# Attention's back steps of a round in one group, retention's two likewise; rotation tiles of q in turn with gate tiles

## What is computed

```python
def second_block(x, ...):
    for l in range(DEPTH_2):
        h = rmsnorm(x, attn_norm[l])
        z = h @ w_in[l]
        (qA, kA, vA, fA, qB, kB, vB, qI, kI, wI,
         qC, kC, vC, gC, qD, kD, vD, gates) = jnp.split(z, split_at, axis=-1)
        yA = forgetting_attention(heads(qA, FOX_HEADS), ...)
        yB = dsa_attention(rope(heads(qB, DSA_HEADS), pos), ...)
        r = retention(rope(heads(qC, RET_HEADS), pos), rope(heads(kC, RET_HEADS), pos) * HEAD_DIM ** -0.5, ...)
        yC = head_groupnorm(r, ret_norm[l]) * jax.nn.silu(gC)
        yD = sliding_window_gqa(rope(heads(qD, SWA_Q_HEADS), pos), ...)
        branch = jnp.einsum('bsnc,ncd->bsnd', jnp.stack([yA, yB, yC, yD], axis=2), w_branch[l])
        merged = jnp.sum(jax.nn.sigmoid(gates) * branch, axis=2)
        x = x + merged @ w_out[l]
        ...
```

## Time and profile before

| | us |
|---|---|
| median of 3 runs | 3758.53 |
| lowest and highest run | 3755.45, 3760.3 |
| the profiled execution, its time | 3764.61 |
| its span in the trace | 3763.2 |

### The profile page before, as it was taken

How to read it: one execution, slowest core, us unless ns; L and a number is a source line. 1 busy time by engine, 2 the same in 40 slices (tenths; PEclk the granted TensorE clock), 3 DMA queues, 4 the chain that set the end, 5 groups by cost and what they waited for, 6 DMA issues and landing times.

```text
span 3763.2 us, 45163 instructions
## 1 busy us (share of the span) xinstructions
PE 3535.7 (94%) x17424; PEld 2778.0 (74%) x17424; DVE 1708.2 (45%) x3133; ACT 1465.7 (39%) x2478; POOL 1419.3 (38%) x651
## 2 busy tenths in 40 slices
PE   6999989897899998999999999998989999989998
PEld 4788889785578876767766778887866766678886
DVE  6876453547420116845542243134755552334133
ACT  3223454554432223344443344343335443334342
POOL 3454433321234443323332344444323332334443
PEclk9999999999999998999999999999999999999999
DMA  7574445221123331212122222323212222223332
GB/s 287 195 249 145 129 155 163 68 85 51 45 80 94 101 93 62 78 45 68 62 82 70 90 73 90 101 93 99 73 51 62 62 68 85 79 79 90 101 94 80
DMA packets 109975, 364.90 MB, mean 97 GB/s; under 512 B 12609, under 2 KB 13505, under 8 KB 109505
## 3 DMA queue, kind: packets, MB, share of 16 engines
q1 hardware_dynamic: 107280, 356.33, 29.5%
q10 hardware_dynamic: 2480, 5.68, 0.4%
HBM read 359.86 MB, written 2.10 MB: 96 GB/s over the span
## 4 chain that ended last, share of the span: by engine, by line
PE 77%; DVE 14%; ACT 5%; issue 2%; DMA 1%; POOL 1%; SPq 0%; DVEq 0%; POOLq 0%; ACTq 0%
PE ps L1308 24%; PE ps L1310 22%; PE ps L1309 22%; PE ps L1552 1%; PE ps L1573 1%; ACT b L1636 1%; DVE b L2171 1%; DVE b L2464 1%; PE ps L1534 1%; DVE b L2463 1%; DVE b L2207 1%; DVE b L2152 1%; POOL b L2535 1%; PE ps L1530 1%; DVE b L2437 1%
## 5 line engine op out<-in xcount | busy, mean ns | idle before, releaser
L2535 POOL TENSOR_TENSOR b<-b,b 128x1024 fp32r<-128x1024 f32 (+2 forms) x579 | 1325.5, 2289 | 2056.2 <-ACT b L1636 2051.1
L1308 PE MATMUL ps<-b,b 128*128 128x512 f32 (+3 forms) x4848 | 1865.9, 385 | 88.9 <-POOL b L2535 26.7
L1310 PE MATMUL ps<-b,b 128*128 128x512 f32 (+3 forms) x4848 | 1804.4, 372 | 0.0
L1309 PE MATMUL ps<-b,b 128*128 128x512 f32 (+3 forms) x4848 | 1804.0, 372 | 0.0
L1308 PEld LDWEIGHTS ps<-b,b 128*128 128x128 f32 x4848 | 934.3, 193 | 357.5 <-issue 147.5
L1310 PEld LDWEIGHTS ps<-b,b 128*128 128x128 f32 x4848 | 934.5, 193 | 161.5
L1309 PEld LDWEIGHTS ps<-b,b 128*128 128x128 f32 x4848 | 936.7, 193 | 145.5 <-issue 5.0
L1636 ACT ACTIVATE b<-b 128x1024 fp32r<-128x1024 f32 (+2 forms) x622 | 607.4, 978 | 269.9 <-PE ps L1310 239.1
L2075 DVE SCALAR_TENSOR_TENSOR b<-ps,b,b 128x511 f32<-128x511 f32 x88 | 66.0, 750 | 371.0 <-ACT b L1687 371.0
L1697 ACT ACTIVATE b<-b 128x512 fp32r<-128x512 f32 (+1 forms) x110 | 64.8, 589 | 391.6 <-DVE b L2084 289.2
L2171 DVE CUSTOM_DVE_ANT_0 b<-b,b,b 128x1024 bf16<-128x1024 f32 x112 | 209.4, 1870 | 17.5 <-DMA b<-in_ada 5.5
(11 more groups left out here) (235 smaller groups left out, 2380.5 us busy)
## 6 DMA issues: line engine op xcount, KB each, us to landing
b<-in_w SPq DMA_DIRECT2D x458, 512.0 KB, 3.5
b<-in_ada SPq DMA_DIRECT2D x88, 512.0 KB, 4.9
b<-in_w SPq DMA_DIRECT2D x80, 384.0 KB, 3.1
b<-in_w SPq DMA_DIRECT2D x80, 320.0 KB, 2.9
b<-in_const SPq DMA_DIRECT2D x24, 256.0 KB, 4.0
b<-in_x SPq DMA_DIRECT2D x1, 2048.0 KB, 16.7
out<-b SPq DMA_DIRECT2D x8, 256.0 KB, 2.5
b<-in_c SPq DMA_DIRECT2D x2, 512.0 KB, 10.1
```

What stands on the lines that cost most here:

```text
L1308: pe.matmul(out, a[0], b[0], start=first, stop=False)
L1309: pe.matmul(out, a[0], b[1], start=False, stop=False)
L1310: return pe.matmul(out, a[1], b[0], start=False, stop=last)
L2535: then(pool.tensor_tensor(wlo[j % NS][:, 0:nk * w], raw[j % NR][:, 0:nk * w], whi[j % NS][:, 0:nk * w].bitcast(F32), ALU.subtract), "lop", j)
```

## The change

Three things are edited. First, the back steps of a round are one item of the list: heads() returns a list [s3, s2, s1] for each round, retention a list [c2, c1], and weave() puts such a list in whole. Second, the rates are changed for that: from 0.8 to 0.31 in A, from 0.6 to 0.235 in B and D, from 0.55 to 0.35 in C, so that a group comes after every fifth k-step in A, every sixth or seventh in B and D, and every fourth or fifth in C, where before single steps came after every second or third. rn1 and rn2 stay single items. Third, in A two gate tiles and one rotated tile of q alternate, four times over, where before four rotated tiles came first; plan() orders the chunks the same way.

```diff
-                cols("gt", w2, l, GT, 1024)
...
-        cols("qb", w2, l, QB, 512)
+        for m in range(4):
+            cols("gt", w2, l, GT + 256 * m, 256)
+            cols("qb", w2, l, QB + 128 * m, 128)
         branch(0)
...
-    def rope(self, name, count, key, **kw):
-        for m in range(count):
+    def rope(self, name, count, key, at=0, **kw):
+        for m in range(at, at + count):
...
-    out, due, back = [], 0.0, list(back)
+    out, due, back = [], 0.0, [b if isinstance(b, list) else [b] for b in back]
...
             if back:
-                out.append(back.pop(0))
-    return out + back
+                out += back.pop(0)
+    return out + [s for b in back for s in b]
...
             for k in range(len(PAIRS) + 3):
-                if k >= 3:
-                    out.append(do("s3", a=kind, l=l, w=k - 3))
-                if 0 <= k - 2 < len(PAIRS):
-                    out.append(do("s2", a=kind, l=l, w=k - 2))
-                if k < len(PAIRS):
-                    out.append(do("s1", a=kind, l=l, w=k))
+                out.append([do(s, a=kind, l=l, w=w) for s, w in (("s3", k - 3), ("s2", k - 2), ("s1", k))
+                            if 0 <= w < len(PAIRS)])
...
-        F.rope("qb", 4, "qb", ver=H, l=l)
-        for m in range(8):
-            t = F.fm("gt", m, "gt", H, L, o=0, l=l)
-            F.step("evac", t=t)
-        S += weave(F, heads("A"), 0.8) + [do("takey", l=l, o=0, t=t) for t in range(4)]
+        for m in range(12):
+            if m % 3 == 2:
+                F.rope("qb", 1, "qb", at=m // 3, ver=H, l=l)
+            else:
+                t = F.fm("gt", m - m // 3, "gt", H, L, o=0, l=l)
+                F.step("evac", t=t)
+        S += weave(F, heads("A"), 0.31) + [do("takey", l=l, o=0, t=t) for t in range(4)]
...
-        S += weave(F, heads("B"), 0.6) + [do("takey", l=l, o=1, t=t) for t in range(4)]
+        S += weave(F, heads("B"), 0.235) + [do("takey", l=l, o=1, t=t) for t in range(4)]
...
-            if k >= 2:
-                B.append(do("c2", l=l, w=k - 2))
-            if k < len(PAIRS):
-                B.append(do("c1", l=l, w=k))
+            B.append([do(c, l=l, w=w) for c, w in (("c2", k - 2), ("c1", k)) if 0 <= w < len(PAIRS)])
```

More of the change, by code:

```diff
@@ L517, in schedule @@
         branch(F, 1, 1)
-        S += weave(F, heads("D"), 0.6) + [do("takey", l=l, o=2, t=t) for t in range(4)]
+        S += weave(F, heads("D"), 0.235) + [do("takey", l=l, o=2, t=t) for t in range(4)]
         F = fore()
@@ L523, in schedule @@
         for k in range(len(PAIRS) + 2):
-            if k >= 2:
-                B.append(do("c2", l=l, w=k - 2))
-            if k < len(PAIRS):
-                B.append(do("c1", l=l, w=k))
+            B.append([do(c, l=l, w=w) for c, w in (("c2", k - 2), ("c1", k)) if 0 <= w < len(PAIRS)])
             if k >= 2 and (k - 2) % 4 == 3:
                 B += [do("rn1", l=l, t=(k - 2) // 4), do("rn2", l=l, t=(k - 2) // 4)]
-        S += weave(F, B, 0.55) + [do("takey", l=l, o=3, t=t) for t in range(4)]
+        S += weave(F, B, 0.35) + [do("takey", l=l, o=3, t=t) for t in range(4)]
         F = fore()
```

## The result

| | us |
|---|---|
| before, median of 4 runs | 3759.41 (3755.45 to 3763.25) |
| after, median of 4 runs | 3826.51 (3824.40 to 3829.37) |
| after / before | 1.017, 95% interval 1.0155 to 1.0185 |
| span of the profiled execution | 3827.9 (before 3763.2) |

The change makes the kernel slower, by 67 us. The forecast was 3802 us with a range from 3768 to 3828: the sign and the mechanism held, the size was 24 us short, and the time lies only 1.5 us inside the upper end.

The account below looks back on a forecast made before the run. Stages were taken as bound by TensorE's issue (busy 94%), leaving only idle time to gain. Per layer 24 + 4 - 2.7 - 4.1 = +21 us, two layers +43 us on the median 3758.5: 3802 us, range 3768 to 3828.

Parts of the forecast that it names:

- rival 3: Slower still: B's starting lag also hits next q tiles' banks and D's start, clock falls every wait; 3826 us, chance 0.08.
- the lag at B's start: The last q rotation, 3.5 us on VectorE, now ends A and delays B; claimed to run through two rotations.
- Where s2 stands: A, B, D: s2 waits for scalings behind rotation parts; 14.4 to 38.5 us, +24 us a layer, bounds 8 and 32.
- R + 4.1: Earliest s2 start behind two to four rotation parts; R: later of tile's end + 0.8 and last maximum + 1.3.
- rival 1: Cover: VectorE reaches the scaling sooner, so new waits vanish and A's go too; -11 us a layer, 3736 us, chance 0.10.
- B's start: First s2 wait in B, behind the last q rotation and takey's subtractions: 3.0 or 7 us, taken as 6.
- Branch tiles: B and D: waits of s2 behind a tile's products (2.9 us) and for its bank (0.9) unchanged: 0, +-3 us.
- The clock: Half-clock stretches after long waits: 13 us lost against 9.5, +4 us a layer, bounds -4 and +12.
- Grouping by itself: s3, s2, s1 in a row save nothing; c2 beside c1 saves a shape change, -2.7 us a layer.
- Rival 2: Format switching: each step away from split fp32 tiles costs, so grouping gives 13 us a layer more; 3776 us, chance 0.06.
- Retention: Stage C: waits before c2's first round and before rn1 and rn2 vanish, -4.1 us; shape changes give -2.7 us.
- A's waits: Sign of being right: waits in stage A near 8 us a layer, against 13.3 before.

Follow-up runs that it names:

- early scaling: The changed kernel with VectorE's scaling of pair k-1 issued directly behind the maximum of s1 of pair k: 3710.4 us.
- short GpSimd operation: The changed kernel with GpSimd's subtraction cut to 16 columns for weight chunks split while a rotated tile's parts run on VectorE: 3767.1 us.
- head steps grouped only: The kernel before with only s3, s2, s1 of a round grouped, at the new spacing; old order of tiles and of retention: 3841.5 us.
- q first: The changed kernel with each q tile of A ahead of its two gate tiles, so a gate tile ends the stage: 3821.8 us.
- single steps and early scaling: The kernel before, old tile order, with the scaling of pair k-1 issued directly behind the maximum of s1 of pair k: 3723.5 us.

## Why the prediction was right, and where it was short

**How near to the edge.** The prediction's own range was 3775 to 3825, and 3826.5 lies outside it; it is inside 3828 only because half of rival 3 had been let in. That rival's 3826 is the measured time, in part by luck. Of what it named, the clock falling at more waits is what came; the lag at B's start hit one bank (1.5 us), and D's start waited no longer than forecast (4.2 us against 4.3).

**Where s2 stands: right, place by place.** The forecast for layer 0 was waits of 3.3, 2.0, 2.6 us in A; measured 3.1, 2.0, 1.8. In B 6.0, 2.5, 3.0, 1.2, 2.2, 2.4, 2.7 were forecast; measured 4.9, 2.3, 2.8, 1.3, 2.5, 1.8, 0.7. In D 4.3, 2.9, 3.4; measured 4.2, 2.7, 2.7. Together 38.5 against 32.9. The rule "R + 4.1" from the earlier trace rows carried over to stages in which the kernel before had no such wait. The experiments with early scaling and with the short GpSimd operation show both halves of its cause, the place and the hold by GpSimd. The cover of rival 1 was not there: its 18 undisturbed scalings all stood behind a finished rotation and with s1 elsewhere.

**B's start: right in sum, with another split.** 6 us were put on the first s2. It waited 4.9 us, and a tile's first matmul 1.5 us just ahead, for the bank that the lagging parts still read. The second wait of this kind (2.1 us, at the value tile) stood nowhere in the sum; it isn't rival 3's lag, since it stays where no rotation ends A (2.1 us with head steps grouped only and with q first, where the 1.5 us are gone).

**Branch tiles: a term taken as nothing.** "Keep their number in the order; I take 0, +-3" was wrong by the upper bound and more: before 3.8 us with the tile's bank, after 1.0 and 1.5 us in B and 2.3, 1.2 and 2.2 us in D (each with the second head's 0.2), 8.2 us. The timeline of one in D, the same pattern without a rotation: the tanh (L1752) behind the exponentials, an addition to the merged result (L2126) that waits for GpSimd, then the scaling.

```profile
1922.59 0.49 ACT L1926 ACTIVATE b<-b,b 128x256 f32<-128x256 f32 x1
...
1923.26 0.57 ACT L1752 ACTIVATE b<-ps 128x512 f32<-128x512 f32 x1
...
1924.93 2.37 POOL L2532 TENSOR_TENSOR b<-b,b 128x1024 fp32r<-128x1024 f32 x1 [4.23 <-ACT b L1633]
1925.55 2.30 DVE L2126 TENSOR_TENSOR b<-b,b 128x512 f32<-128x512 f32 x1
...
1928.15 0.35 DVE L2434 TENSOR_SCALAR b<-b,b 128x256 f32<-128x256 f32 x1
...
1928.56 0.44 PE L1549 MATMUL ps<-b,b 128*128 128x128 f32 x2 [2.06 <-DVE b L2434]
```

I had counted rotation parts only. In a branch tile this other VectorE addition, held by GpSimd too (2.30 us), does the same.

**The clock: the term that was mis-sized.** Forecast +4 us a layer, 13 lost instead of 9.5. Measured: 58 us at half clock instead of 20.5. The loss of 0.454 us for each us of such a stretch, worked out from the earlier trace rows, makes 26 us instead of 9, so about +17, above the bound of +12 (+16.4 if TensorE's idle time inside the stretches, 2.7 us and 1.3 before, is left out). Two things were wrong. Only waits of 2.4 us and more were counted, eight or nine stretches; but stretches stand also behind waits of 2.0 and 1.8 us in A (the row 1640.00:1643.20 below), and at B's 1.8, 2.1 and 2.3 and D's 2.1. And each was taken as 3.4 us long; four last 6.8 us, as the 1718.50:1725.20 above does.

```profile
1640.00:1643.20 3.20, 3.20 (x12) 2.28 (x9) 2.08 (x8) 1.51 (x5) 0.00 (x0) 0.50 0.30 116
```

That is 13 us a layer more than forecast, and by size it is all of the 24 us (12 a layer) that were missing; layer 1, with 58.0 instead of 17.1 us at half clock, lost no less. The other misses nearly cancel: the forecast waits came out 5.6 us too long, the ones not in the sum (banks 3.6, s1 0.8, branch tiles 8.2 less 3.8) are 8.8 us, and the steps themselves, below, gave back 4.8 us more than forecast.

**Grouping by itself.** Rival 2 would have shown in s1 standing 0.1 us behind s2, the forecast in a full 0.2. The timeline of PE in A, a pair that doesn't wait:

```profile
1590.56 0.39 PE L1307 MATMUL ps<-b,b 128*128 128x512 f32 x1
1590.79 0.38 PE L1549 MATMUL ps<-b,b 128*128 128x128 f32 x2
1591.10 0.92 PE L1527 MATMUL ps<-b,b 64*128 64x384 f32 x4
```

The second transpose stands at 1590.79 + 0.11 = 1590.90, and s1 0.20 behind it, where a third transpose would have come after 0.11: the change of shape costs 0.09 us here too. But the round as a whole gains a little. Where nothing waits, at full clock, s3, s2 and s1 as one group take TensorE 0.07 us less than the three single steps between fore matmuls (eight, four and four matmuls, s1 with 256 columns: 0.79, 0.45 and 0.84 us singly in the kernel before, 2.00 together in the one with early scaling), and the layer with only the heads grouped comes out some 5 us shorter than before without its waits and its half clock (4.6 and 4.7 us in the two layers, between the same two fore matmuls): nearer to the 0 of the forecast than to the 13 us of rival 2. Why it isn't 0, with as many changes of shape as before, stays open. The Trainium skill (TensorEngine Tiling (Array Packing), "Key Properties") says that a change of the tiling mode drains TensorE; these rows agree, with 0.09 us where the shape changes.

**Retention: right.** -4.1 us of waits were forecast and -4.4 measured, -2.7 for the shape and -3.0 measured by rows (-4 with what has no shown cause).

**The sum.** Per layer: idle time +23.9 us (forecast 24 - 4.1, about 20), half clock +17 (forecast 4), steps -7.5 (forecast -2.7), together +33.4 (forecast +21), where the steps are what is left of the measured time. The two layers in the trace, 31 and 33 us longer, leave some -9 for the steps. The two runs with one grouping each give -4 for retention and -5 for the heads by the same count, so nothing of size is unassigned. A's waits came as forecast (7.3 against "near 8"), C got shorter by more (10 us against 5 to 8).

## What to carry to other kernels

When steps of a pipeline are put together, follow the other engines: what a step leaves on ScalarE and VectorE (here maxima and exponentials) moves with it, ahead of whatever those engines owed the next step. Here the cure was not a better place for TensorE's steps but to issue the one small VectorE operation (the scaling) as soon as its input is there, a round ahead of its reader. And price the clock with the waits: here each us of new idle time went with another 0.7 us lost to the half clock (17 beside 23.9).

## What the hardware showed that I had not expected

- The granted clock fell to half at waits of PE as short as 1.8 us (A's third, B's sixth), and stayed at 1.00 at others of 1.0 to 1.5 us and at one of 2.0 us in D (1985.6). In the kernel with single steps and early scaling a wait of 3.0 us in A left it at 1.00 in layer 0. So the length of a wait alone doesn't tell whether the clock falls; what else decides stays open.
- The lock by GpSimd reaches operations of one column: in D an addition of 128x1 (L2432) took 0.99 us at 1879.27, with a GpSimd subtraction running from 1877.90 for 2.34 us, where the shortest take 0.15.

```profile
1877.90 2.34 POOL L2532 TENSOR_TENSOR b<-b,b 128x1024 fp32r<-128x1024 f32 x1
1879.27 0.99 DVE L2432 TENSOR_TENSOR b<-b 128x1 f32<-128x1 f32 x1
```
